# Four of eight output tiles stay in PSUM from one feed-forward round to the next

## The chip, the cores and the metric

One core of a Trainium2 chip runs the whole kernel. The metric is device time in microseconds (us). Five engines take part: TensorE (PE in the profile: matmuls; PEld is its weight load), VectorE (DVE), ScalarE (ACT), GpSimd (POOL) and SyncE (SP), which issues the loads of weights. Each has its own queue of instructions and runs it in order; they wait for each other by semaphores. Matmuls write to PSUM, which has eight banks of 512 float32 values per partition; `k.bank[0]` to `k.bank[7]` here.

## What is computed

Two blocks of a transformer on 512 tokens of width 1024, in float32: an "even" and an "odd" mixer, then a chain with four feed-forward stages and two mixers between them. Only the feed-forward stages (`ffn00`, `ffn01`, `ffn10`, `ffn11`) are touched:

```python
def swiglu(x, w_in, w_out):                       # w_in 1024 x 5632, w_out 2816 x 1024
    gate, up = jnp.split(x @ w_in, 2, axis=-1)
    return (jax.nn.silu(gate) * up) @ w_out
...
h = layer_norm(DN_ALPHA * h + 0.5 * swiglu(h, ffn_w_in[i, 0], ffn_w_out[i, 0]), ln_g[i, 0], ln_b[i, 0])
```

## The kernel before

**Precision.** Every float32 operand is held as a high part and the rest (`w_hi`, `w_lo`, `h_hi`, `h_lo`, ...), and each product is three matmuls (lines 368 to 370, or 448 to 450 for the output): high by high, high by rest, rest by high. ScalarE makes the high part by a copy, VectorE the rest by a subtraction of the high part from the value.

**Rounds.** A feed-forward stage goes over its 2816 hidden features in 11 rounds of 256 (`ROUNDS`). Round r has three pieces of weights: "a" and "b" (each 128 gate and 128 up columns of `w_in`) and "o" (256 rows of `w_out`). TensorE's order is a(r), b(r), and then the output of the round before, o(r-1). From round 2 (`SEVEN`) on, each of a and b is done by seven products of half-sized blocks instead of eight (`PRODUCTS`, `tensor_seven`): products x = 0 to 6, each of 12 matmuls of 256 columns, into banks 0 to 3. The weights that such a product takes come in three units: A22, A1 (blocks A11 and A12), and S, four sums of blocks. GpSimd makes the sums in four instructions (`gpsimd_sums`, lines 1076, 1078, 1079 and 1081, in this order), ScalarE their high part (line 1106), VectorE the rest in two halves (`vector_unit_s`, line 1130), and the second half raises `w_s`. GpSimd starts on the next piece's sums when the `w_s` of the piece before is raised and its weights have landed. `vector_unit_a22` is line 1123, `vector_unit_a1` line 1140.

**Between the products** VectorE adds partial results: `vector_mid` (lines 1150, 1153, and 1156 with 1157), `vector_c11` (1163), `vector_c12` (1169) and `vector_products` (1177, and 1182 twice). TensorE's product 4 waits for line 1150 (`f_u`), product 5 for line 1153 (`f_e`), product 6 for lines 1156 and 1157 (`f_g`). Line 1049 is the rest of one of four sums of the activations, made once a stage (`vector_t_rest`).

**The output.** `tensor_out` makes o(r) as eight tiles j of 128 tokens by 512 columns (`OUTS`), in banks 4 to 7: tile j in bank 4 + j % 4. A tile is six matmuls of 512 columns, three for each half of the hidden features. It first does the first half for tiles 0 to 3, then the second half tile by tile, and tiles 4 to 7 entirely, each after the tile before it in its bank has been taken out. VectorE takes each tile out and adds it onto `acc` (`vector_out`, line 544; line 542 in the round that also multiplies by ALPHA). The last two rounds of a stage (9 and 10) are made by `tensor_exit` on top of tiles copied back into PSUM. Neither it nor round 8's eight takes change.

**The order of VectorE's queue** is written out by hand in `vector_ffn` and `vector_seventh`. The places where tiles 4 to 7 are taken out are these:

```python
    vector_t_rest(k, stage, "T1")                       # vector_ffn, before round 2
    vector_outs_ffn(k, stage, 0, range(4, 8))
    vector_seventh(k, stage)                            # begins with vector_unit_a22, vector_mid, ...
...
    vector_unit_a22(k, n)                               # vector_seventh, before round 3
    vector_outs_ffn(k, stage, r - 1, range(4, 8))
    vector_unit_s(k, n, 0)
```

Of the kernel before, what the change touches and what calls it, by code (L numbers as in the profile page):

```python
# [24 lines left out]
ROUNDS = DFF // 256  # L25
# [93 lines left out]
PIECES = _pieces()  # L119
AT = {p: n for n, p in enumerate(PIECES)}  # L120
# [49 lines left out]
def seeded(n, j=0):  # L170


    stage, what, i = PIECES[n]
    if stage[:3] == "ffn":
        return what == "o" and i >= ROUNDS - 2
    last = i >= NH - 2 if stage == "gla" else i == NH - 1
    return stage in SEEDED and what in ("out", "oa", "ob") and last and j in SEEDED[stage]


def gated(n):  # L180
# [259 lines left out]
def out_part(k, n, j, c, first, last, hi, lo):  # L440
    return out_tile(k, n, j, c, k.bank[4 + j % 4][:], first, last, hi, lo)


def out_tile(k, n, j, c, o, first, last, hi, lo):
    t, half = OUTS[j]
    onto = seeded(n, j)
    x, w = slice(t * P, (t + 1) * P), slice(c * D + half * T, c * D + (half + 1) * T)
    k.nc.tensor.matmul(o, hi[:, c, x], k.hi(n)[:, w], start=first and not onto, stop=False, skip_group_check=onto)  # L448
    k.nc.tensor.matmul(o, lo[:, c, x], k.hi(n)[:, w], start=False, stop=False, skip_group_check=onto)  # L449
    return k.nc.tensor.matmul(o, hi[:, c, x], k.lo(n)[:, w], start=False, stop=last, skip_group_check=onto)  # L450


def tensor_out(k, n, ready, free, order=(0, 1), hi=None, lo=None):


    pe = k.nc.tensor
    hi, lo = (k.oh_hi, k.oh_lo) if hi is None else (hi, lo)
    pe.wait_ge(*k.at("w_lo", n))
    pe.wait_ge(*k.at(*ready[0]))
    for j in range(4):  # L460
        pe.wait_ge(*k.at(*free[j]))
        out_part(k, n, j, order[0], True, False, hi, lo)
    pe.wait_ge(*k.at(*ready[1]))
    for j in range(8):
        if j >= 4:
            pe.wait_ge(*k.at("acc", (n, j - 4)))
            out_part(k, n, j, order[0], True, False, hi, lo)
        ins = out_part(k, n, j, order[1], False, True, hi, lo)
        ins.then_inc(*(k.up("out", (n, j)) if j < 7 else k.up("used", n)))


def tensor_exit(k, B, n, ready, free, turn, free_turn, order=(0, 1), x=None, n0=None, ready0=(), x0=None):
# [56 lines left out]


def out_done(n, j):
    return ("out", (n, j)) if j < 7 else ("used", n)


def vector_out(k, n, j, alpha=False, bank=None):


    t, half = OUTS[j]
    dst, b = k.acc[:, t, half * T:(half + 1) * T], k.bank[4 + j % 4 if bank is None else bank][:]
    k.nc.vector.wait_ge(*k.at(*out_done(n, j)))  # L540
    if alpha:
        ins = k.nc.vector.scalar_tensor_tensor(dst, dst, ALPHA, b, MULT, ADD)
    else:
        ins = k.nc.vector.scalar_tensor_tensor(dst, b, 1.0, dst, MULT, ADD)  # L544
    ins.then_inc(*k.up("acc", (n, j)))
# [573 lines left out]
def vector_unit_a22(k, n):  # L1119
    ve = k.nc.vector  # L1120
    ve.wait_ge(*k.at("u_hi", (n, "A22")))
    hi, lo = (wide_view(x) for x in w_blocks(k, n, "A22", 1))
    ve.tensor_tensor(lo, raw_block(k, n, 1, 1), hi.bitcast(F32), SUB)
# [11 lines left out]
def vector_unit_a1(k, n):  # L1135

    ve = k.nc.vector
    ve.wait_ge(*k.at("u_hi", (n, "A1")))
    hi, lo = (wide_view(x) for x in w_blocks(k, n, "A1", 2))
    ve.tensor_tensor(lo, a1_raw(k, n), hi.bitcast(F32), SUB).then_inc(*k.up("w_lo", n))  # L1140
# [19 lines left out]
def vector_c11(k, stage, r, s):  # L1160
    ve, key, p1 = k.nc.vector, (stage, r, s), k.f_h[:, s, HALF[0]]
    ve.wait_ge(*k.at("f_p", key + (4,)))
    ve.tensor_tensor(p1, p1, k.bank[1][:, 0:256], ADD).then_inc(*k.up("f_c11", key))  # L1163
# [139 lines left out]
def vector_seventh(k, stage):  # L1303


    r = SEVEN
    n, n_o = AT[stage, "b", r], AT[stage, "o", r - 1]
    vector_unit_a22(k, n)
    vector_mid(k, stage, r, 0, 0)
    vector_mid(k, stage, r, 0, 1)  # L1310
    vector_unit_a1(k, n)
    vector_mid(k, stage, r, 0, 2)
    vector_c11(k, stage, r, 0)
    vector_unit_s(k, n, 0)
    vector_unit_s(k, n, 1)
    vector_c12(k, stage, r, 0)
    vector_piece_half(k, n_o, 0)
    vector_products(k, stage, r, 0)
    k.nc.vector.wait_ge(*k.at("f_h", (stage, r, 0)))
    vector_mid(k, stage, r, 1, 0)  # L1320
    vector_hidden_split(k, stage, r, 0)
    vector_mid(k, stage, r, 1, 1)
    vector_piece_half(k, n_o, 1)
    vector_mid(k, stage, r, 1, 2)
    n = AT[stage, "a", r + 1]
    vector_unit_a22(k, n)
    vector_c11(k, stage, r, 1)
    vector_c12(k, stage, r, 1)
    vector_products(k, stage, r, 1)
    vector_unit_s(k, n, 0)  # L1330
    vector_unit_s(k, n, 1)
    vector_hidden_split(k, stage, r, 1)
    vector_outs_ffn(k, stage, r - 1, range(2))
    vector_unit_a1(k, n)
    vector_outs_ffn(k, stage, r - 1, range(2, 4))
    n = AT[stage, "b", r + 1]
    vector_unit_a22(k, n)
    vector_outs_ffn(k, stage, r - 1, range(4, 8))
    vector_unit_s(k, n, 0)
    vector_unit_s(k, n, 1)  # L1340


def vector_ffn(k, stage):
    ve, B = k.nc.vector, FFN_NEXT[stage]
    vector_piece(k, AT[stage, "a", 1])
    ve.wait_ge(*k.at("h_lo", (stage, 1, 3)))
    vector_t_sum(k, stage, "T1")
    ve.wait_ge(*k.at("t_sum", (stage, "T1")))
    vector_t_sum(k, stage, "T2")
    vector_t_rest(k, stage, "T2")  # L1350
    vector_hidden(k, stage, 0, 0)
    vector_piece(k, AT[stage, "b", 1])
    vector_hidden_split(k, stage, 0, 0)
    ve.wait_ge(*k.at("t_lo", (stage, "T2")))
    vector_t_sum(k, stage, "T4")
    vector_t_rest(k, stage, "T4")
    vector_hidden(k, stage, 0, 1)
    vector_hidden_split(k, stage, 0, 1)
    vector_piece(k, AT[stage, "o", 0])
    ve.wait_ge(*k.at("t_lo", (stage, "T4")))  # L1360
    vector_t_sum(k, stage, "T3")
    vector_t_rest(k, stage, "T3")
    vector_hidden(k, stage, 1, 0)
    n = AT[stage, "a", SEVEN]
    vector_unit_a22(k, n)
    vector_hidden_split(k, stage, 1, 0)
    vector_hidden(k, stage, 1, 1)
    vector_outs_ffn(k, stage, 0, range(2))
    vector_unit_s(k, n, 0)
    vector_outs_ffn(k, stage, 0, range(2, 3))  # L1370
    vector_hidden_split(k, stage, 1, 1)
    vector_outs_ffn(k, stage, 0, range(3, 4))
    vector_unit_s(k, n, 1)
    vector_unit_a1(k, n)
    vector_t_rest(k, stage, "T1")
    vector_outs_ffn(k, stage, 0, range(4, 8))
    vector_seventh(k, stage)
    for r in range(SEVEN + 1, ROUNDS):
        last = r == ROUNDS - 1
        vector_mid(k, stage, r, 0, 0)  # L1380
        vector_piece(k, AT[stage, "o", r - 1])
        vector_mid(k, stage, r, 0, 1)
        vector_mid(k, stage, r, 0, 2)
        vector_unit_a1(k, AT[stage, "b", r])
        vector_c11(k, stage, r, 0)
        vector_c12(k, stage, r, 0)
        vector_products(k, stage, r, 0)
        vector_hidden_split(k, stage, r, 0)
        n = None if last else AT[stage, "a", r + 1]
        if not last:  # L1390
            vector_unit_a22(k, n)
        vector_mid(k, stage, r, 1, 0)
        vector_mid(k, stage, r, 1, 1)
        if last:
            vector_piece(k, AT[stage, "o", r])
        else:
            vector_unit_s(k, n, 0)
        vector_mid(k, stage, r, 1, 2)
        if not last:
            vector_unit_s(k, n, 1)  # L1400
        vector_c11(k, stage, r, 1)
        vector_c12(k, stage, r, 1)
        vector_products(k, stage, r, 1)
        vector_hidden_split(k, stage, r, 1)
        if not last:
            vector_outs_ffn(k, stage, r - 1, range(2))
            vector_unit_a1(k, n)
            vector_outs_ffn(k, stage, r - 1, range(2, 4))
            n = AT[stage, "b", r + 1]
            vector_unit_a22(k, n)  # L1410
            vector_unit_s(k, n, 0)
            vector_outs_ffn(k, stage, r - 1, range(4, 6))
            vector_unit_s(k, n, 1)
            vector_outs_ffn(k, stage, r - 1, range(6, 8))
        elif B != "end":
            vector_piece(k, HEAD[B][0])
            vector_piece(k, HEAD[B][1])
    vector_exit(k, B, AT[stage, "o", ROUNDS - 1])


def vector_outs_ffn(k, stage, r, outs):
    for j in outs:
        vector_out(k, AT[stage, "o", r], j, r == 0)


def sync_final(k):
# [2511 lines left out]
```

## Time and profile before

| | |
|---|---|
| time, median of 3 runs (lowest, highest) | 2694.2 us (2692.37, 2696.44) |
| time of the profiled execution | 2693.18 us |
| its span, first to last instruction | 2691.6 us |
| mean granted clock of TensorE | 0.997 |
| busy: PE, PEld | 2646.5 us (98%), 2303.0 us (86%) |
| busy: VectorE, ScalarE, GpSimd | 1937.9 us (72%), 1123.7 us (42%), 577.0 us (21%) |
| takes of line 544 and line 542 | 374 and 48 |

Times of rows are us from the start of the span. A row of the timeline gives start, duration, engine and line, and what it writes and reads; a number in brackets is the idle time of the engine before it and what ended it. Of a feed-forward stage's three pieces, products run on lines 368 to 370 of PE and outputs on lines 448 to 450.

### The profile page before, as it was taken

To read this page: it belongs to the slowest core of one execution; us is meant where nothing else is said; L and a number is where in the kernel's file an instruction comes from. 1 tells how busy PE (TensorE), PEld (TensorE's weight loads), DVE (VectorE), ACT (ScalarE), POOL (GpSimd) and SP (SyncE) were. 2 spreads that over 40 slices of the span, in tenths; PEclk is the share of its full clock that TensorE was granted. 3 is DMA by queue.
4 is the path that set the end of the run, shared out by engine and by line. 5 is a ranking of instruction groups with operands and counts; after the bars stand their busy time and mean duration, and the time that the engine had idled before them with its cause. 6 is when DMAs were issued, how large, how long until landed. Compare 5 with 4: busy or idle time off the path is not lost.

```text
span 2691.6 us, 38695 instructions
## 1 busy us (share of the span) xinstructions
PE 2646.5 (98%) x15901; PEld 2303.0 (86%) x15901; DVE 1937.9 (72%) x2651; ACT 1123.7 (42%) x1624; POOL 577.0 (21%) x366
## 2 busy tenths in 40 slices
PE   9899999999999999999999999999999999999998
PEld 6787877678899997888999988999988888889997
DVE  7888634656888865448888778888655745788876
ACT  4444555543433445353434444434432332444343
POOL 2211000101444400001544214444000000044440
PEclk9999999999999999999999999999999999999999
DMA  9543222212333332222333323333323223233331
GB/s 303 157 150 107 63 63 63 79 52 78 122 94 106 99 110 66 92 63 73 116 97 121 108 72 121 95 107 98 110 83 110 78 72 110 78 108 97 94 110 63
DMA packets 297891, 268.34 MB, mean 100 GB/s; under 512 B 11047, under 2 KB 265265, under 8 KB 297586
## 3 DMA queue, kind: packets, MB, share of 16 engines
q1 hardware_dynamic: 294050, 256.99, 30.9%
q0 software_dynamic: 2368, 6.64, 0.7%
q8 instruction: 126, 2.06, 0.3%
q10 hardware_dynamic: 1296, 2.23, 0.3%
q14 instruction: 51, 0.42, 0.0%
HBM read 263.72 MB, written 2.10 MB: 99 GB/s over the span
## 4 chain that ended last, share of the span: by engine, by line
PE 81%; DVE 12%; ACT 3%; issue 3%; POOL 1%; DMA 0%; DVEq 0%; POOLq 0%; ACTq 0%
PE psum L368 14%; PE psum L370 14%; PE psum L369 14%; PE psum L448 7%; PE psum L449 7%; PE psum L450 7%; PE psum L424 2%; PE psum L425 2%; PE psum L426 2%; PE psum L3040 1%; DVE w_lo L353 1%; DVE w_lo L1130 1%; PE psum L3053 1%; PE psum L1621 1%; PE psum L2608 1%
## 5 line engine op out<-in xcount | busy, mean ns | idle before, releaser
L368 PE MATMUL psum<-h_hi,w_hi 128*128 128x256 f32 (+1 forms) x2224 | 720.0, 324 | 12.8 <-DVE consts L1153 4.2
L370 PE MATMUL psum<-h_hi,w_lo 128*128 128x256 f32 (+1 forms) x2224 | 701.8, 316 | 0.0
L369 PE MATMUL psum<-h_lo,w_hi 128*128 128x256 f32 (+1 forms) x2224 | 701.4, 315 | 0.0
L368 PEld LDWEIGHTS psum<-h_hi,w_hi 128*128 128x128 f32 x2224 | 425.5, 191 | 47.7 <-issue 9.7
L369 PEld LDWEIGHTS psum<-h_lo,w_hi 128*128 128x128 f32 x2224 | 425.5, 191 | 28.4 <-issue 4.8
L370 PEld LDWEIGHTS psum<-h_hi,w_lo 128*128 128x128 f32 x2224 | 425.1, 191 | 27.0
L1076 POOL TENSOR_TENSOR val<-w_raw 128x512 f32<-128x512 f32 x72 | 100.4, 1395 | 963.5 <-DMA w_raw<-in_ffn_w_in 567.9
L353 DVE TENSOR_TENSOR w_lo<-w_raw,w_hi 128x2048 fp32r<-128x2048 f32 x98 | 223.1, 2287 | 83.4 <-ACT w_hi L348 77.3
L544 DVE SCALAR_TENSOR_TENSOR acc<-psum,acc 128x512 f32<-128x512 f32 x374 | 242.2, 679 | 36.0 <-PE psum L450 35.4
L368 PE MATMUL psum<-t_hiffn,w_hi 128*128 128x256 f32 x864 | 244.9, 283 | 0.4
L369 PE MATMUL psum<-t_loffn,w_hi 128*128 128x256 f32 x864 | 244.5, 283 | 0.0
L370 PE MATMUL psum<-t_hiffn,w_lo 128*128 128x256 f32 x864 | 244.5, 283 | 0.0
L348 ACT ACTIVATE w_hi<-w_raw 128x2048 fp32r<-128x2048 f32 x102 | 193.3, 1910 | 65.9 <-PE psum L450 57.2
L1200 ACT ACTIVATE consts<-consts 128x256 f32<-128x256 f32 x144 | 58.2, 418 | 294.6 <-DVE consts L1163 270.0
L1130 DVE TENSOR_TENSOR w_lo<-val,w_hi 128x1024 fp32r<-128x1024 f32 x144 | 174.1, 1216 | 9.4 <-ACT w_hi L1106 8.5
L368 PEld LDWEIGHTS psum<-t_hiffn,w_hi 128*128 128x128 f32 x864 | 165.8, 192 | 1.3 <-DVE f_cffn L1157 1.3
L369 PEld LDWEIGHTS psum<-t_loffn,w_hi 128*128 128x128 f32 x864 | 165.9, 192 | 0.0
L370 PEld LDWEIGHTS psum<-t_hiffn,w_lo 128*128 128x128 f32 x864 | 165.9, 192 | 0.0
L1079 POOL TENSOR_TENSOR val<-w_raw 128x512 f32<-128x512 f32 x72 | 161.4, 2241 | 0.0
L1106 ACT ACTIVATE w_hi<-val 128x2048 fp32r<-128x2048 f32 x72 | 138.0, 1916 | 38.0 <-POOL val L1081 31.2
L348 ACT ACTIVATE w_hiffn<-w_raw 128x2048 fp32r<-128x2048 f32 x40 | 76.5, 1913 | 128.3 <-PE psum L450 128.3
L448 PE MATMUL psum<-w_hiffn,f_oh_hiffn 128*128 128x512 f32 x320 | 125.6, 393 | 0.0
(460 smaller groups left out, 5603.0 us busy)
## 6 DMA issues: line engine op xcount, KB each, us to landing
w_raw<-in_ffn_w_in SPq DMA_DIRECT2D x176, 512.0 KB, 5.0
w_raw<-in_ffn_w_out SPq DMA_DIRECT2D x88, 512.0 KB, 6.2
w_raw<-in_ret_w_in SPq DMA_DIRECT2D x48, 512.0 KB, 4.6
ada_raw<-in_ada_w SPq DMA_DIRECT2D x32, 512.0 KB, 4.4
w_raw<-in_odd_w_in SPq DMA_DIRECT2D x32, 512.0 KB, 4.8
w_raw<-in_even_w_in SPq DMA_DIRECT2D x24, 512.0 KB, 6.1
w_raw<-in_gla_w_in SPq DMA_DIRECT2D x24, 512.0 KB, 4.8
ada_first<-in_ada_w SPq DMA_DIRECT2D x32, 256.0 KB, 6.2
```

Of the source, the lines that this page charges most:

```text
L348: k.nc.scalar.activation(k.hi(n), k.w_raw[:, buffer(n), :], ACT.Copy).then_inc(*k.up("w_hi", n))
L353: k.nc.vector.tensor_tensor(k.lo(n), k.w_raw[:, buffer(n), :], k.hi(n).bitcast(F32), SUB).then_inc(*k.up("w_lo", n))
L368: k.nc.tensor.matmul(out, ws, xs, start=first, stop=False)
L369: k.nc.tensor.matmul(out, ws, xl, start=False, stop=False)
L370: return k.nc.tensor.matmul(out, wl, xs, start=False, stop=last)
L448: k.nc.tensor.matmul(o, hi[:, c, x], k.hi(n)[:, w], start=first and not onto, stop=False, skip_group_check=onto)
L449: k.nc.tensor.matmul(o, lo[:, c, x], k.hi(n)[:, w], start=False, stop=False, skip_group_check=onto)
L450: return k.nc.tensor.matmul(o, hi[:, c, x], k.lo(n)[:, w], start=False, stop=last, skip_group_check=onto)
L544: ins = k.nc.vector.scalar_tensor_tensor(dst, b, 1.0, dst, MULT, ADD)
L1079: po.tensor_tensor(sum_block(k, "S3"), a11, a21, ADD).then_inc(*k.pool.up())
L1106: sc.activation(w_blocks(k, n, "S", 4)[0], k.sums, ACT.Copy).then_inc(*k.up("u_hi", (n, "S")))
L1130: ins = ve.tensor_tensor(lo, k.sums[:, x], hi.bitcast(F32), SUB)
```

## The change

Tiles of o(0) to o(7) are no longer all taken out. Each of these rounds leaves the last four tiles that it made in banks 4 to 7. The next round makes the same four tiles first and adds onto what lies there, so tiles alternate: round 0 goes 0 to 7 and keeps 4 to 7; round 1 goes 4 to 7, then 0 to 3, and keeps 0 to 3; and so on. VectorE takes out the first four of a round, in the same places of its queue as before, and four takes a round fall away for eight rounds. Round 8 begins with the four that were kept and has all eight taken out. TensorE's waits for the take of a kept tile fall away too. No matmul is added or removed.

```diff
--- before.py
+++ after.py
@@ -177,6 +177,23 @@
     return stage in SEEDED and what in ("out", "oa", "ob") and last and j in SEEDED[stage]
 
 
+def kept(r):
+
+    return r < ROUNDS - 3
+
+
+def out_order(n):
+
+    stage, what, r = PIECES[n]
+    return (4, 5, 6, 7, 0, 1, 2, 3) if stage[:3] == "ffn" and what == "o" and r < ROUNDS - 2 and r % 2 else tuple(range(8))
+
+
+def onto_kept(n, j):
+
+    stage, what, r = PIECES[n]
+    return stage[:3] == "ffn" and what == "o" and 0 < r < ROUNDS - 2 and kept(r - 1) and j in out_order(n)[:4]
+
+
 def gated(n):
     return PIECES[n][0] in ("even", "odd") and PIECES[n][1] == "out"
 
@@ -443,7 +460,7 @@
 
 def out_tile(k, n, j, c, o, first, last, hi, lo):
     t, half = OUTS[j]
-    onto = seeded(n, j)
+    onto = seeded(n, j) or onto_kept(n, j)
     x, w = slice(t * P, (t + 1) * P), slice(c * D + half * T, c * D + (half + 1) * T)
     k.nc.tensor.matmul(o, hi[:, c, x], k.hi(n)[:, w], start=first and not onto, stop=False, skip_group_check=onto)
     k.nc.tensor.matmul(o, lo[:, c, x], k.hi(n)[:, w], start=False, stop=False, skip_group_check=onto)
@@ -457,16 +474,18 @@
     hi, lo = (k.oh_hi, k.oh_lo) if hi is None else (hi, lo)
     pe.wait_ge(*k.at("w_lo", n))
     pe.wait_ge(*k.at(*ready[0]))
-    for j in range(4):
-        pe.wait_ge(*k.at(*free[j]))
+    tiles = out_order(n)
+    for j in tiles[:4]:
+        if not onto_kept(n, j):
+            pe.wait_ge(*k.at(*free[j % 4]))
         out_part(k, n, j, order[0], True, False, hi, lo)
     pe.wait_ge(*k.at(*ready[1]))
-    for j in range(8):
-        if j >= 4:
-            pe.wait_ge(*k.at("acc", (n, j - 4)))
+    for j in tiles:
+        if j not in tiles[:4]:
+            pe.wait_ge(*k.at("acc", (n, j ^ 4)))
             out_part(k, n, j, order[0], True, False, hi, lo)
         ins = out_part(k, n, j, order[1], False, True, hi, lo)
-        ins.then_inc(*(k.up("out", (n, j)) if j < 7 else k.up("used", n)))
+        ins.then_inc(*k.up(*out_done(n, j)))
 
 
 def tensor_exit(k, B, n, ready, free, turn, free_turn, order=(0, 1), x=None, n0=None, ready0=(), x0=None):
@@ -529,7 +548,7 @@
 
 
 def out_done(n, j):
-    return ("out", (n, j)) if j < 7 else ("used", n)
+    return ("out", (n, j)) if j != out_order(n)[-1] else ("used", n)
 
 
 def vector_out(k, n, j, alpha=False, bank=None):
@@ -1335,7 +1354,6 @@
     vector_outs_ffn(k, stage, r - 1, range(2, 4))
     n = AT[stage, "b", r + 1]
     vector_unit_a22(k, n)
-    vector_outs_ffn(k, stage, r - 1, range(4, 8))
     vector_unit_s(k, n, 0)
     vector_unit_s(k, n, 1)
 
@@ -1373,7 +1391,6 @@
     vector_unit_s(k, n, 1)
     vector_unit_a1(k, n)
     vector_t_rest(k, stage, "T1")
-    vector_outs_ffn(k, stage, 0, range(4, 8))
     vector_seventh(k, stage)
     for r in range(SEVEN + 1, ROUNDS):
         last = r == ROUNDS - 1
@@ -1409,9 +1426,11 @@
             n = AT[stage, "b", r + 1]
             vector_unit_a22(k, n)
             vector_unit_s(k, n, 0)
-            vector_outs_ffn(k, stage, r - 1, range(4, 6))
+            if not kept(r - 1):
+                vector_outs_ffn(k, stage, r - 1, range(4, 6))
             vector_unit_s(k, n, 1)
-            vector_outs_ffn(k, stage, r - 1, range(6, 8))
+            if not kept(r - 1):
+                vector_outs_ffn(k, stage, r - 1, range(6, 8))
         elif B != "end":
             vector_piece(k, HEAD[B][0])
             vector_piece(k, HEAD[B][1])
@@ -1419,8 +1438,9 @@
 
 
 def vector_outs_ffn(k, stage, r, outs):
+    n = AT[stage, "o", r]
     for j in outs:
-        vector_out(k, AT[stage, "o", r], j, r == 0)
+        vector_out(k, n, out_order(n)[j], r < 2 and j < 4)
 
 
 def sync_final(k):
```

## Rows read from the trace of the kernel before

**Rows 1.** The page: busy time of TensorE, and the costliest group of takes.

```profile
PE 2646.5 (98%) x15901; PEld 2303.0 (86%) x15901; DVE 1937.9 (72%) x2651; ACT 1123.7 (42%) x1624; POOL 577.0 (21%) x366
...
L544 DVE SCALAR_TENSOR_TENSOR acc<-psum,acc 128x512 f32<-128x512 f32 x374 | 242.2, 679 | 36.0 <-PE psum L450 35.4
```

**Rows 2.** Windows of ffn01: products of rounds 2, 3 and 4; length, busy times, clock, DMA.

```profile
1275.21:1296.74 21.53, 20.87 (x169) 20.39 (x169) 20.80 (x28) 10.07 (x12) 13.52 (x10) 1.00 0.57 164
...
1307.65:1329.37 21.72, 20.66 (x170) 20.25 (x168) 17.62 (x24) 9.86 (x12) 9.74 (x7) 1.00 0.33 103
...
1340.28:1360.43 20.15, 20.15 (x170) 20.15 (x168) 15.28 (x24) 8.21 (x11) 9.93 (x6) 1.00 0.36 112
```

**Rows 3.** TensorE's waits over the whole run: total us, times, longest.

```profile
PE psum L368 <- DVE consts L1153: 4.2, 4, 1.1
...
PE psum L368 <- DVE f_cffn L1150: 2.3, 4, 0.7
```

**Rows 4.** Timeline of TensorE in ffn01, at three places of rounds 2 and 3.

```profile
1279.51 0.28 PE L370 MATMUL psum<-h_hi,w_lo 128*128 128x256 f32 x1
...
1291.85 0.39 PE L368 MATMUL psum<-h_hi,w_hi 128*128 128x256 f32 x1 [0.54 <-DVE f_cffn L1150]
...
1316.04 0.39 PE L368 MATMUL psum<-h_hi,w_hi 128*128 128x256 f32 x1 [1.04 <-DVE consts L1153]
```

**Rows 5.** Timeline of VectorE in ffn01, start of round 2.

```profile
1275.08 2.33 DVE L1049 TENSOR_TENSOR h_lo<-lng,h_hi 128x1024 fp32r<-128x1024 f32 x1
1277.33 2.47 DVE L542 SCALAR_TENSOR_TENSOR acc<-acc,psum 128x512 f32<-128x512 f32 x4
1279.72 0.68 DVE L1123 TENSOR_TENSOR w_lo<-w_raw,w_hi 128x512 fp32r<-128x512 f32 x1
1280.32 0.41 DVE L1150 TENSOR_TENSOR f_cffn<-consts,psum 128x256 f32<-128x256 f32 x1
1280.83 0.42 DVE L1153 TENSOR_TENSOR consts<-f_cffn,psum 128x256 f32<-128x256 f32 x1
1281.17 1.47 DVE L1140 TENSOR_TENSOR w_lo<-w_raw,w_hi 128x1024 fp32r<-128x1024 f32 x1
...
1283.56 2.35 DVE L1130 TENSOR_TENSOR w_lo<-val,w_hi 128x1024 fp32r<-128x1024 f32 x2
```

**Rows 6.** Timeline of GpSimd in the same stretch.

```profile
1274.16 2.16 POOL L1076 TENSOR_TENSOR val<-w_raw 128x512 f32<-128x512 f32 x1 [24.10 <-DVE w_lo L1130]
1276.40 2.17 POOL L1078 TENSOR_TENSOR val<-val,w_raw 128x512 f32<-128x512 f32 x1
1278.53 1.31 POOL L1079 TENSOR_TENSOR val<-w_raw 128x512 f32<-128x512 f32 x1
1279.92 1.64 POOL L1081 TENSOR_TENSOR val<-val,w_raw 128x512 f32<-128x512 f32 x1
```

**Rows 7.** Timeline of ScalarE in the same stretch.

```profile
1281.59 1.92 ACT L1106 ACTIVATE w_hi<-val 128x2048 fp32r<-128x2048 f32 x1 [0.34 <-POOL val L1081]
```

**Rows 8.** Timeline of VectorE in ffn01, later in round 2.

```profile
1291.38 0.42 DVE L1150 TENSOR_TENSOR f_cffn<-consts,psum 128x256 f32<-128x256 f32 x1
```

**Rows 9.** Timeline of VectorE in ffn01, from o(1) into round 3.

```profile
1305.08 2.10 DVE L544 SCALAR_TENSOR_TENSOR acc<-psum,acc 128x512 f32<-128x512 f32 x3
1307.85 0.69 DVE L544 SCALAR_TENSOR_TENSOR acc<-psum,acc 128x512 f32<-128x512 f32 x1 [0.67 <-PE psum L450]
1309.68 2.36 DVE L1130 TENSOR_TENSOR w_lo<-val,w_hi 128x1024 fp32r<-128x1024 f32 x2 [1.14 <-ACT w_hi L1106]
...
1312.29 3.36 DVE L353 TENSOR_TENSOR w_loffn<-w_raw,w_hiffn 128x2048 fp32r<-128x2048 f32 x1
```

**Rows 10.** Timeline of GpSimd in ffn01: the last sum for round 3.

```profile
1306.41 1.29 POOL L1081 TENSOR_TENSOR val<-val,w_raw 128x512 f32<-128x512 f32 x1
```

**Rows 11.** Timelines of VectorE and GpSimd in ffn01, into round 4.

```profile
1343.35 0.42 DVE L1150 TENSOR_TENSOR f_cffn<-consts,psum 128x256 f32<-128x256 f32 x1 [0.87 <-PE psum L370]
...
1341.65 1.32 POOL L1076 TENSOR_TENSOR val<-w_raw 128x512 f32<-128x512 f32 x1 [8.51 <-DMA w_raw<-in_ffn_w_in]
```

## Prediction

> **What bounds the kernel now.** I read the page first. TensorE's matmuls are busy for 98% of the span [rows 1], so the question is where TensorE stands still in the four feed-forward stages; only such time can be given back, since the change leaves every matmul in place. All matmuls of one size follow each other at one fixed spacing, so a stretch of TensorE with a known count of matmuls has a known length, and what is over it is a stall. I cut ffn01 into windows at the points where TensorE goes from lines 368-370 to 448-450 and back. The products of round 4 take 20.15 us, with TensorE busy all the time; the timeline of the later rounds looks the same. Round 2 takes 21.53 us and round 3 21.72 us for the same products [rows 2]. So a stage loses 1.38 us in round 2 and 1.57 us in round 3, 2.95 us, some 12 us in four stages. The waits of TensorE confirm who is late: lines 1150 and 1153 of VectorE, four times each, once a stage [rows 3]. In the timeline the first is product 4 of b in round 2, which waits for line 1150, the second product 5 of a in round 3, which waits for line 1153 [rows 4].
>
> **What is removed, and what it is worth by itself.** Eight rounds of four takes in four stages are 128 takes at 0.679 us [rows 1], 87 us of VectorE's time. In rounds 4 to 10 TensorE doesn't wait, so nothing comes of it there. The takes matter only in so far as they make VectorE late for the two stalls. Both have four of them somewhat ahead in VectorE's queue.
>
> **Round 3 first.** VectorE's last take ends at 1307.85 + 0.69 = 1308.54. Then it stands still for 1.14 us until ScalarE has made the high part of S, and starts on S at 1309.68 [rows 9]. ScalarE had waited for GpSimd's last sum, which runs from 1306.41 to 1307.70 in 1.29 us, under takes [rows 10]; its other durations in this stage are 1.31 us at the least and 2.17 us at the most [rows 6]. So takes don't slow GpSimd, and without them S would start at 1309.68 all the same. The next piece, line 353, is held to 3.36 us and is what makes line 1153 late [rows 9, 4]; it comes behind S and doesn't move. Removing the four takes here is worth 0: what hides them is the wait for GpSimd's sums.
>
> **Round 2.** Here four takes at 1277.33 to 1279.80 stand between line 1049 and line 1123 [rows 5]. They are covered in the same way: S starts at 1283.56 [rows 5], 0.05 us after ScalarE's line 1106 has ended at 1281.59 + 1.92 = 1283.51, which began 0.03 us after GpSimd's last sum ended at 1279.92 + 1.64 = 1281.56 [rows 6, 7]. So also here the earlier VectorE gains nothing past S. The sums themselves, however, can get later.
>
> Look at how the two engines run against each other. GpSimd's 1076 takes 2.16 us, 1078 2.17, 1079 1.31 and 1081 1.64 [rows 6]. 1079 is the one that runs wholly beside takes. 1078 was issued at 1276.40 while VectorE's line 1049 was running until 1275.08 + 2.33 = 1277.41, and ended 1.16 us after that. Line 1049 in turn was issued while GpSimd's 1076 ran until 1276.32, and ended 1.09 us after that, though the same shape on line 1130 takes 2.35 / 2 [rows 5]. So the two do not share: a subtraction of VectorE that reads two operands from SBUF and a sum of GpSimd run one after the other, and they take turns, where both stand ready. A take, which reads one operand from PSUM, doesn't count, and nor do lines 1150 and 1153.
>
> The Trainium skill says it so ("SBUF — State Buffer", "Who interferes with whom"): VectorE and GpSimd share a port pair under an exclusive lock for the whole instruction, and a VectorE instruction with two SBUF inputs contends with a GpSimd instruction that reads SBUF, one with at most one SBUF input doesn't. The trace agrees with it: 1.31 us beside takes, 2.17 us beside line 1049. This rule speaks against the change: the takes are a stretch in which GpSimd has the port for itself. The same page ("A bandwidth-pool intuition that's wrong") gives some 115 ns from the end of the one to the start of the other, for a DMA issue held by a copy; with three handovers more on GpSimd's way (below) that would be an estimate of 0.35 us a stage, and the sum 1.4 us higher.
>
> Now without the takes, step by step for ffn01:
> - line 1123 is issued at 1277.33, just as GpSimd's 1078 has got its turn, which it holds until 1276.40 + 2.17 = 1278.57. An instruction that was held ends its own length less 0.13 us after the other (1.22 against 1.09 for line 1049), so 1123 ends at 1278.57 + 0.68 - 0.13 = 1279.12.
> - 1079 is issued at 1278.53 as before, is now held by 1123, and ends 1.16 us after it, at 1280.28. Before: 1279.84.
> - line 1150 runs from 1279.04. Line 1153 needs product 2, whose last matmul starts at 1279.51 and lasts 0.28 us [rows 4]. So it starts at some 1279.83, and line 1140 is issued 0.34 us later, at 1280.17. 1081 can't be issued before 1280.36 (1079's end and the 0.08 us seen between them now). So 1140 is next in turn and ends 1.09 us after 1079, at 1281.37.
> - 1081 ends 1.16 us after that, at 1282.53, in place of 1281.56: 0.97 us later.
> - ScalarE's 1106 follows 0.03 us later, and S 0.05 us after it: 1284.53 in place of 1283.56.
>
> Behind S in VectorE's queue stand line 1169, half of line 360, 1177, 1182 twice and line 1150 at 1291.38 [rows 8], which TensorE has waited for since product 3 of b was issued; GpSimd's next sums are started by the end of S, so they move with it and meet the same instructions. None of these waits for TensorE, and nothing between gives the time back. So line 1150 and TensorE's restart at 1291.85 [rows 4] move by 0.97 us, and all that follows in the stage moves with TensorE. Three other stages have the same order and the same durations. **Sum:** 4 x 0.97 = +3.9 us.
>
> **The other parts of the change.** Accumulating in place of overwriting: the second half of each tile accumulates today at the same spacing, so 0. The other order of tiles: the same 48 matmuls, the first four of a round still taken in the same places, so 0. The waits dropped for kept tiles: these takes ended at 1308.54, 20 us before the next output at 1329.37, so 0 (its cover is a whole round). From round 4 on S ends some 1.2 us earlier, which raises `w_s` earlier; but GpSimd's first sum waits for its weights to land (1341.65, after 8.51 us), and line 1150 waits for TensorE (1343.35) [rows 11]. So these meet as before: 0. Below nothing I see no cost here, unless the load lands earlier than I read it, which is a rival below.
>
> **Against the measured time.** The profiled execution took 2693.18 us with a span of 2691.6 us, 1.6 us around it; it is 1.0 us below the median of 2694.2 us. I add the sum to the median: **2698.1 us**. A difference under 0.2% (5.4 us) is about what a measurement of this kernel can't tell from no change, and the forecast lies within it.
>
> **Rivals.**
> - *The turn falls the other way* (0.22). Line 1140 is issued only 0.19 us ahead of 1081. If it comes later, 1081 goes first and ends 1.25 us after its issue at 1280.36, at 1281.61 in place of 1281.56. Then nothing moves: 2694.2 us, within 1. For it speaks how small the margin is, against it that all of it hangs on TensorE's regular spacing.
> - *The stalls go* (0.12), the case on the other side. If what holds S back is VectorE's lateness and not the sums, then VectorE comes to both places 2.4 us earlier (four takes of 2.47 us), more than either stall. All of it: -4 x 2.95 = -11.8 us, 2682.4 us (0.04). Only round 3's: -4 x 1.57 = -6.3 us, 2687.9 us (0.05); less than that, 2691 us (0.03). It decides from where the sums end more than 1 us ahead of VectorE's arrival at S. Against it stand the 0.03 and 0.05 us of rows 5 to 7 and the 1.14 us of idle time in rows 9.
> - *A new collision in rounds 4 to 10* (0.08). If the weights land early enough that GpSimd starts 1.2 us sooner, its sums meet line 353 in another phase, and a whole sum of 1.3 us can come ahead of it. In rows 11 GpSimd is let go by the load, so it is unlikely. The price lies between 0 and the 1.31 us of a sum; TensorE has some slack in these rounds, so I take 0.5 us, in six rounds of four stages +12 us: 2706 us. It decides from line 1153 being later than product 4 of a takes.
> - *The forecast* (0.58): 2695.5 to 2700.5 us, the handovers' price being the unknown.
>
> **How the numbers follow.** The range reaches from the half-way gains to the forecast's upper end with some of the costly case: 2689 to 2702 us. Faster by over 0.2%: the first two parts of the second rival, 0.09. Slower by over 0.2%: the third rival and the upper edge of the forecast, 0.08 + 0.08 = 0.16. Within: 0.75.
>
> **What the profile after would show.** If right: 246 takes of line 544 in place of 374 (and 48 of line 542, as now, since round 1's first four are scaled in place of round 0's last); line 1079 of round 2 at some 1.75 us in place of 1.31, and 1081 at 2.2 in place of 1.64; S of round 2 a microsecond later against TensorE's start of the round; products of round 2 at 22.5 us, of round 3 at 21.7, of round 4 at 20.15. It is wrong if round 3's products fall to 20.2 us, or if round 2's stay at 21.5 us.

## The result and the profile after

The changed kernel takes 2698.49 us (median of 20 runs, 2694.35 to 2701.92) against 2694.38 us for the kernel before (20 runs, 2691.77 to 2697.28). The ratio is 1.0016, with a 95% interval of 1.0009 to 1.0023: slower by 4.1 us, forecast +3.9.

The page of the changed kernel: its VectorE line, and the group of takes.

```profile
PE 2651.5 (98%) x15901; PEld 2306.7 (85%) x15901; DVE 1867.4 (69%) x2523; ACT 1122.5 (42%) x1624; POOL 581.1 (22%) x366
...
L563 DVE SCALAR_TENSOR_TENSOR acc<-psum,acc 128x512 f32<-128x512 f32 x246 | 160.1, 680 | 32.8 <-PE psum L467 32.7
```

VectorE is busy for 70.5 us less than in [rows 1], with 128 instructions fewer, and TensorE makes the same 15901 matmuls. (The 128 takes lasted 87 us, but the rows of neighbouring takes overlap a little, and VectorE's other instructions last 6.3 us longer in all: one that is held by another engine counts as busy.) The kernel is slower all the same. Windows of the same three stretches of ffn01 say where; columns as in [rows 2].

```profile
1279.33:1301.84 22.51, 21.13 (x170) 20.48 (x169) 19.43 (x24) 9.85 (x12) 14.47 (x10) 1.00 0.53 159
1312.75:1334.20 21.45, 20.40 (x169) 20.20 (x168) 16.56 (x23) 9.74 (x12) 9.65 (x7) 1.00 0.33 105
1345.14:1365.29 20.15, 20.15 (x169) 20.15 (x168) 13.34 (x22) 8.18 (x11) 9.92 (x6) 1.00 0.37 115
```

Round 2 has grown from 21.53 to 22.51 us, round 4 is 20.15 us as it was. Cut in the same way, round 2 takes 22.50, 22.51, 22.50 and 22.49 us in the four stages, 3.7 us more in all than the 21.66, 21.53, 21.57 and 21.55 us before. Round 3 gives 0.3 us back in one stage. TensorE's waits over the whole run:

```profile
PE psum L385 <- DVE f_cffn L1169: 5.0, 4, 1.3
PE psum L385 <- DVE consts L1172: 4.2, 4, 1.0
```

Lines 1169 and 1172 are lines 1150 and 1153 of before. The wait for the first has gone from 2.3 to 5.0 us in total, that for the second has stayed at 4.2 us [rows 3]. The rows of waits show less than the windows do (2.7 against 3.7 us), since a part of each stall counts as busy: for the same matmuls of round 2 the busy time has gone from 20.87 to 21.13 us. The windows are what I go by. The profiled execution of the changed kernel took 2701.88 us, 8.7 us more than that of before, and only 3.4 us of this lie in rounds 2 and 3. Another 3.3 us lie ahead of the first instruction that differs (its round 2 of ffn00 begins at 689.20 us, before at 685.94 us), and 1.9 us between round 3 of ffn10 and round 2 of ffn11, where TensorE's granted clock fell to 1.2 GHz for some 3 us in this execution (the last section shows it). A single pair of spans would have told more than twice the truth; medians and stretches of fixed work agree.

**How the microsecond is lost.** VectorE in ffn01, start of round 2, after:

```profile
1279.19 2.34 DVE L1068 TENSOR_TENSOR h_lo<-lng,h_hi 128x1024 fp32r<-128x1024 f32 x1
1281.45 1.78 DVE L1142 TENSOR_TENSOR w_lo<-w_raw,w_hi 128x512 fp32r<-128x512 f32 x1
1283.16 0.41 DVE L1169 TENSOR_TENSOR f_cffn<-consts,psum 128x256 f32<-128x256 f32 x1
1283.95 0.42 DVE L1172 TENSOR_TENSOR consts<-f_cffn,psum 128x256 f32<-128x256 f32 x1 [0.39 <-PE psum L387]
1284.29 1.22 DVE L1159 TENSOR_TENSOR w_lo<-w_raw,w_hi 128x1024 fp32r<-128x1024 f32 x1
...
1286.83 0.42 DVE L1182 TENSOR_TENSOR consts<-consts,psum 128x256 f32<-128x256 f32 x1 [0.67 <-PE psum L387]
1288.64 2.36 DVE L1149 TENSOR_TENSOR w_lo<-val,w_hi 128x1024 fp32r<-128x1024 f32 x2 [1.39 <-ACT w_hi L1125]
...
1296.46 0.42 DVE L1169 TENSOR_TENSOR f_cffn<-consts,psum 128x256 f32<-128x256 f32 x1
```

GpSimd and ScalarE beside it, and TensorE at product 4 of b:

```profile
1280.52 2.16 POOL L1097 TENSOR_TENSOR val<-val,w_raw 128x512 f32<-128x512 f32 x1
1282.65 1.77 POOL L1098 TENSOR_TENSOR val<-w_raw 128x512 f32<-128x512 f32 x1
1284.50 2.17 POOL L1100 TENSOR_TENSOR val<-val,w_raw 128x512 f32<-128x512 f32 x1
```

```profile
1286.70 1.91 ACT L1125 ACTIVATE w_hi<-val 128x2048 fp32r<-128x2048 f32 x1 [1.33 <-POOL val L1100]
```

```profile
1296.93 0.39 PE L385 MATMUL psum<-h_hi,w_hi 128*128 128x256 f32 x1 [1.24 <-DVE f_cffn L1169]
```

Line 1142 (1123 before) has the same work as in [rows 5] and lasts 1.78 us in place of 0.68, because it stands behind sum 1097. The third sum lasts 1.77 us in place of 1.31, behind line 1142, and the fourth 2.17 us in place of 1.64, behind line 1159. VectorE, which was busy almost without a gap up to S before, now stands still for 0.39, for 0.67 and, ahead of S, for 1.39 us, and S is still later. The removed work was replaced by waiting, and the waiting is longer.

### The profile page after: what moved, and what is told of

Same layout as the page of the kernel before. It is cut to its first block, busy times and chain, and to the rows that moved or that the text cites. A ratio compares the mean times of both kernels' runs of the same rounds, so it can differ in the third digit from the quotient of the medians.

```text
span 2700.3 us, 38567 instructions
## 1 busy us (share of the span) xinstructions
PE 2651.5 (98%) x15901; PEld 2306.7 (85%) x15901; DVE 1867.4 (69%) x2523; ACT 1122.5 (42%) x1624; POOL 581.1 (22%) x366
## 4 chain that ended last, share of the span: by engine, by line
PE 79%; DVE 12%; ACT 4%; issue 3%; POOL 2%; DMA 0%; DVEq 0%; SPq 0%; POOLq 0%; ACTq 0%
PE psum L385 13%; PE psum L387 13%; PE psum L386 13%; PE psum L465 7%; PE psum L466 7%; PE psum L467 7%; PE psum L443 2%; PE psum L441 2%; PE psum L442 2%; DVE w_lo L370 1%; PE psum L3060 1%; DVE w_lo L1149 1%; PE psum L3073 1%; PE psum L1641 1%; PE psum L2628 1%
## 5 line engine op out<-in xcount | busy, mean ns | idle before, releaser
L563 DVE SCALAR_TENSOR_TENSOR acc<-psum,acc 128x512 f32<-128x512 f32 x246 | 160.1, 680 | 32.8 <-PE psum L467 32.7
```

## Experiments

Two theories of the loss. **A**, that of the prediction: in round 2 GpSimd's sums lose turns to VectorE's subtractions, since the four takes beside which they ran undisturbed are gone. **B**: every kept round costs TensorE a little, by accumulating onto a bank or by the other order of tiles; 4.1 us over 32 kept rounds is 0.13 us each, too little to be told from a few products. They differ in where the loss sits and in whether it can be undone with all kept tiles in place.

**Only round 0 keeps tiles** (`e1`). In every later round all eight tiles are taken out as before, though the odd rounds stay in the other order of tiles:

```diff
 def kept(r):
-    return r < ROUNDS - 3
+    return r == 0
...
 def evacuated(n):
-    return [("acc", (n, 4 + j)) for j in range(4)]
+    return [("acc", (n, out_order(n)[4 + j])) for j in range(4)]
...
     vector_unit_a22(k, n)                               # vector_seventh, before round 3
+    vector_outs_ffn(k, stage, r - 1, range(4, 8))
     vector_unit_s(k, n, 0)
```

> Only round 0 of each stage keeps its last four tiles; round 1 makes them first and then all eight are taken out, and the later rounds are as before. Theory A (the sums of round 2 lose their turns at the port once the four takes of round 0 are gone): all of the loss is here, +3.9 us against before, products of round 2 at 22.5 us in place of 21.5. Theory B (each kept round costs something on TensorE, by accumulating or by its other order): one of eight kept rounds, +0.5 us, round 2 at 21.5 us.

Measured: 2698.71 us against 2694.91, ratio 1.0013 (1.0005 to 1.0022). Its round 2 in ffn01:

```profile
1277.02:1299.54 22.52, 21.13 (x169) 20.46 (x169) 19.44 (x24) 9.86 (x12) 14.50 (x10) 1.00 0.54 158
```

16 of the 128 removed takes bring the whole loss, as theory A has it.

**All rounds but round 0 keep tiles** (`e2`), with the changed `evacuated` too:

```diff
 def kept(r):
-    return r < ROUNDS - 3
+    return 0 < r < ROUNDS - 3
...
     vector_t_rest(k, stage, "T1")                       # vector_ffn, before round 2
+    vector_outs_ffn(k, stage, 0, range(4, 8))
     vector_seventh(k, stage)
...
-        vector_out(k, n, out_order(n)[j], r < 2 and j < 4)
+        vector_out(k, n, out_order(n)[j], r == 0)
```

> Rounds 1 to 7 keep four tiles, round 0 doesn't: its last four takes are back ahead of round 2. Theory A: no change against before, within 1 us, products of round 2 at 21.5 us and of round 3 at 21.4 to 21.7 us, though 112 of the 128 takes are gone. Theory B: seven of eight kept rounds, +3.6 us.

Measured: 2694.62 us against 2694.91, ratio 1.0000 (0.9991 to 1.0008). Windows of its rounds 2 and 3 in ffn01:

```profile
1274.36:1295.92 21.56, 20.88 (x169) 20.39 (x169) 20.82 (x28) 10.07 (x12) 13.53 (x10) 1.00 0.55 164
1306.83:1328.54 21.71, 20.66 (x169) 20.25 (x168) 16.93 (x23) 9.86 (x12) 9.73 (x7) 1.00 0.33 104
```

Removing the other 112 takes is worth nothing that could be measured, and accumulating onto a kept bank in seven rounds costs nothing either: every output of 48 matmuls takes 10.91 us, as before. Theory B, which asked for 3.6 us, falls. Round 3's own stall is there (21.71 us), though the four takes just ahead of its S are gone: their cover was GpSimd, as [rows 9, 10] said.

**The turns given back, with every tile kept** (`e3`). One line moves in `vector_seventh`:

```diff
-    vector_unit_a22(k, n)
     vector_mid(k, stage, r, 0, 0)
+    vector_unit_a22(k, n)
     vector_mid(k, stage, r, 0, 1)
```

> The changed kernel with one line moved: in round 2 VectorE adds the first partial result (vector_mid 0) ahead of the rest of A22, and no longer behind it. The partial result is ready only when TensorE has done product 1, so the rest of A22 is issued some 0.2 us after GpSimd's third sum and not 1.2 us ahead of it. Theory A: the third sum falls back from 1.77 to 1.3 us, the fourth ends a microsecond earlier, round 2's products return to 21.5 us, and the time to that of before, within 1 us (-4 us against the changed kernel). Theory B: the time stays at +4 us.

Measured: 2694.14 us against 2694.91, ratio 0.9999 (0.9990 to 1.0008). VectorE and GpSimd in its ffn01:

```profile
1276.27 0.42 DVE L1169 TENSOR_TENSOR f_cffn<-consts,psum 128x256 f32<-128x256 f32 x1 [0.99 <-PE psum L387]
1276.60 1.67 DVE L1142 TENSOR_TENSOR w_lo<-w_raw,w_hi 128x512 fp32r<-128x512 f32 x1
```

```profile
1276.40 1.32 POOL L1098 TENSOR_TENSOR val<-w_raw 128x512 f32<-128x512 f32 x1
1277.80 1.64 POOL L1100 TENSOR_TENSOR val<-val,w_raw 128x512 f32<-128x512 f32 x1
```

```profile
1273.08:1294.64 21.56, 20.90 (x170) 20.42 (x169) 19.93 (x24) 10.08 (x12) 13.52 (x10) 1.00 0.56 165
```

VectorE makes the same instructions as in the changed kernel, but line 1142 is now issued 0.20 us after the third sum and not 1.2 us ahead of it. The sums last 1.32 and 1.64 us, as in [rows 6], and round 2 is back at 21.56 us. The order of two instructions carries the whole loss.

**What the idle time can be used for** (`e4`). TensorE waits for what stands in VectorE's queue behind S, and the changed kernel has a hole ahead of S. Half of the subtraction for the output weights fits in:

```diff
     vector_c11(k, stage, r, 0)
+    vector_piece_half(k, n_o, 0)
     vector_unit_s(k, n, 0)
     vector_unit_s(k, n, 1)
     vector_c12(k, stage, r, 0)
-    vector_piece_half(k, n_o, 0)
```

> The changed kernel, with the first half of the rest of the output weights (vector_piece_half 0) moved ahead of S in round 2, into the 2 us in which VectorE now stands still for the sums. Theory A with the chain behind S as what TensorE waits for: S is no later, line 1150 (1169 in the changed kernel) comes some 2.2 us earlier, product 4 of b no longer waits, products of round 2 fall from 22.5 to 20.2 to 20.5 us, and the time to some 2689.5 us, 5 us under before. If VectorE's place behind S isn't what holds TensorE, nothing moves and it stays at +4 us.

Measured: 2691.40 us against 2694.91, ratio 0.9988 (0.9979 to 0.9996), and round 2 at 21.08 us in ffn01. The sign is right, but round 2 was expected at 20.2 to 20.5 us, so some 0.6 to 0.9 us a stage are missing. TensorE in ffn01 at product 6 of b, and what it waited for:

```profile
1293.11 0.28 PE L387 MATMUL psum<-h_hi,w_lo 128*128 128x256 f32 x1
1293.69 0.39 PE L385 MATMUL psum<-t_hiffn,w_hi 128*128 128x256 f32 x1 [0.30 <-DVE f_cffn L1176]
```

```profile
1290.65 0.41 DVE L1172 TENSOR_TENSOR consts<-f_cffn,psum 128x256 f32<-128x256 f32 x1
1290.98 1.99 DVE L377 TENSOR_TENSOR w_loffn<-w_raw,w_hiffn 128x1024 fp32r<-128x1024 f32 x1
1292.90 0.41 DVE L1175 TENSOR_TENSOR f_cffn<-consts,psum 128x256 f32<-128x256 f32 x1
1293.23 0.41 DVE L1176 TENSOR_TENSOR f_cffn<-f_cffn,psum 128x256 f32<-128x256 f32 x1
```

The wait for line 1169 is gone, and the next one behind it shows: the second half (line 377) is held to 1.99 us by a sum and stands ahead of the partial result for product 6. I had followed the chain to product 4 and no further.

**Both halves moved** (`e6`): besides the edit above,

```diff
     vector_mid(k, stage, r, 1, 1)
-    vector_piece_half(k, n_o, 1)
     vector_mid(k, stage, r, 1, 2)
+    vector_piece_half(k, n_o, 1)
```

> The changed kernel with both halves of the rest of the output weights moved in round 2: the first ahead of S, the second behind vector_mid 2 of b. In the run before, with only the first moved, product 6 of b still lost some 0.5 us behind the second half and product 1 of b 0.2 us behind S. If that reading is right, round 2's products take 20.4 us (21.1 with the first half alone, 22.5 without), round 3's stay at 21.4 to 21.7, and the time is some 2690 us, 4.6 us under before. If product 6 waits for something else, 21.1 us stays.

Measured: 2690.44 us against 2695.39, ratio 0.9981 (0.9972 to 0.9990), round 2 at 20.53 us and round 3 at 21.71 us in ffn01, as expected to 0.1 us. What keeps round 2 some 0.4 us above 20.15 us was not followed up.

**Round 3 as well** (`e7`), in the loop of `vector_ffn`:

```diff
         vector_mid(k, stage, r, 0, 0)
-        vector_piece(k, AT[stage, "o", r - 1])
+        n_o, third = AT[stage, "o", r - 1], r == SEVEN + 1
+        if not third:
+            vector_piece(k, n_o)
         vector_mid(k, stage, r, 0, 1)
+        if third:
+            vector_piece_half(k, n_o, 0)
         vector_mid(k, stage, r, 0, 2)
...
         vector_mid(k, stage, r, 1, 0)
+        if third:
+            vector_piece_half(k, n_o, 1)
         vector_mid(k, stage, r, 1, 1)
```

> As the kernel with both halves moved, and in round 3 too line 353 (370) is cut into halves: the first behind vector_mid 1 of a, the second behind vector_mid 0 of b. What made TensorE wait in round 3 was this one long instruction, held by GpSimd's first sum, ahead of the partial result for product 5. Round 3's products fall from 21.4 to 21.7 us to 20.2 to 20.6, round 2's stay at 20.4, and the time is some 2685.5 us, 9 us under before. If VectorE has too much to do in round 3 for another order to help, the wait comes back at a later product and 21.4 us or more stays.

**And the same moves in the kernel before** (`e8`), with all its takes:

> The kernel before (all 128 takes in place) with the same moves in rounds 2 and 3. It says what the kept tiles are worth once VectorE's order is right. If the takes are covered in round 3 and cost at most a little ahead of S in round 2, where the half piece now comes on top of them, round 2's products take 20.6 to 21.0 us and round 3's 20.2 to 20.6, the time is some 2686.5 to 2687.5 us, and the kept tiles are worth 1 to 2 us. If VectorE's load is what counts, round 2 stays above 21.4 us and the gap to the run above is over 4 us.

Measured: `e7` 2686.66 us, ratio 0.9968 (0.9959 to 0.9977); `e8` 2687.22 us, ratio 0.9974 (0.9966 to 0.9983); both against 2695.39 us. Windows of rounds 2 and 3 in ffn01, first `e7`, then `e8`:

```profile
1274.23:1294.73 20.50, 20.45 (x169) 20.28 (x169) 18.45 (x24) 9.88 (x12) 13.99 (x10) 1.00 0.52 160
1305.64:1325.79 20.15, 20.15 (x169) 20.15 (x168) 16.43 (x24) 9.64 (x12) 8.02 (x6) 1.00 0.36 113
```

```profile
1271.96:1292.63 20.67, 20.47 (x169) 20.30 (x169) 19.80 (x28) 10.00 (x12) 13.01 (x10) 1.00 0.59 158
1303.54:1323.69 20.15, 20.15 (x169) 20.15 (x168) 17.12 (x25) 9.62 (x12) 8.03 (x6) 1.00 0.37 114
```

The products of round 3 have lost their stall in both, so VectorE had time enough there for what they wait for; it did it in the wrong order. The windows of the products don't show that a part of the stall has moved behind them. The outputs after round 3, o(2), take longer; here they are before and in `e7`:

```profile
1329.37:1340.28 10.91, 10.91 (x51) 9.02 (x49) 9.98 (x14) 3.91 (x4) 3.69 (x3) 1.00 0.30 84
1325.79:1337.24 11.45, 11.22 (x51) 8.94 (x49) 10.52 (x12) 3.95 (x5) 4.49 (x4) 1.00 0.26 69
```

The two instructions that finish the hidden features (line 1182 before, 1201 in `e7`) now meet GpSimd's sums in another phase and last longer, and a take that TensorE waits for comes later. The first row is of before, the others are of `e7`:

```profile
1330.03 1.96 DVE L1182 SCALAR_TENSOR_TENSOR consts<-consts,f_cffn 128x256 f32<-128x256 f32 x2
...
1326.45 2.84 DVE L1201 SCALAR_TENSOR_TENSOR consts<-consts,f_cffn 128x256 f32<-128x256 f32 x2
1326.25 1.29 POOL L1097 TENSOR_TENSOR val<-val,w_raw 128x512 f32<-128x512 f32 x1
1331.65 0.50 PE L465 MATMUL psum<-w_hiffn,oh_hi 128*128 128x512 f32 x1 [0.23 <-DVE acc L563]
```

It is so in all four stages of both kernels (11.42 to 11.45 us). In `e7` the products of rounds 2 and 3 give back 10.2 us over the four stages, and these outputs take 2.1 us of it again, which leaves 8.2 us. The times say 8.7 us for `e7` and 8.2 us for `e8`. Between the two kernels lie 0.17 us in round 2 of this stage, some 0.7 us over four, which the intervals of their times don't tell apart; 1 to 2 us had been expected. That is about what the kept tiles are worth once the order is right.

## Why the prediction was right, step by step

- **What TensorE can give back.** Windows of equal work showed 2.95 us of stalls in two rounds of a stage, some 12 us in all [rows 2]. `e7` got 1.03 us of round 2 and 1.57 us of round 3 back in ffn01, and its products from round 3 on take 20.15 to 20.21 us, though 0.54 us came back as a stall in the outputs behind round 3. These 12 us were no part of the sum, only of the second rival.
- **The takes are covered in round 3.** Shown by `e2`, where round 3 took 21.71 us without them.
- **The takes are covered in round 2, and what they cover gets later.** The walk through ffn01 can be laid over the trace. From TensorE's first matmul of round 2 (1275.21 before, 1279.33 after), forecast and measured: line 1123 or 1142 ends at 3.91 and 3.90 us; the third sum ends at 5.07 and 5.09; line 1140 or 1159 is issued at 4.96 and 4.96; the fourth sum ends at 7.32 and 7.34; S starts at 9.32 and 9.31; TensorE restarts at 17.61 and 17.60. So the price of a handover, taken from one pair of rows before, carried over.
- **The Trainium skill's rule** ("SBUF — State Buffer", "Who interferes with whom") is what the runs show: where a VectorE subtraction with two SBUF inputs and a GpSimd sum meet, the second does its work after the first (1.78 us for line 1142 in place of 0.68), while a sum beside takes is not slowed (1.29 to 1.31 us in [rows 6, 10]). The estimate by its figure of 115 ns would have given 5.3 us; the measured loss of 4.1 us (the ratio's interval is 2.4 to 6.2 us) doesn't exclude it, but the places above fit the rows' handovers to 0.02 us.
- **The turn that could have fallen the other way.** Line 1159 was issued 0.21 us ahead of the fourth sum, forecast 0.19, in ffn01, and round 2 came out at the longer length in all four stages.
- **Accumulating, tile order, dropped waits, rounds 4 to 10:** all costed at 0, and none shows a cost: `e2` is at the time of before within 0.1%, and all products from round 4 on take 20.15 to 20.21 us. The collision that was a rival there didn't come: GpSimd's first sum still waited for its weights.
- **What was off:** 4 x 0.97 = 3.9 us was taken for four stages with the same durations. Round 2's own windows give 0.84, 0.98, 0.93 and 0.94 us, 3.7 us. In ffn00 before, S had started 8.45 us after TensorE's first matmul and not 8.35, and not because of the sums: ScalarE's high part was done 0.13 us ahead of it, and S stood right behind line 1163, so VectorE itself was late there and there was less to lose. With round 3's 0.3 us taken off, the windows give 3.4 us and the medians 4.1; the interval holds both, and the forecast's 3.9 us lies between them by chance. The first rival's 1.25 us for a sum that isn't held stands in no row either; the shortest is 1.29 us, and nothing hangs on the difference.
- **What the time alone doesn't show.** The stated range, 2689 to 2702 us, also holds the time of no change, and the 0.2% that the prediction took for the limit of what can be told apart was too wide: with 20 runs of each kernel 4.1 us stood clear of 0. What bears the mechanism out is the walk above and `e1` to `e3`.

## What to carry to other kernels

An instruction off the critical path may be keeping another one away from a shared resource. Before work is taken out of a queue, read what runs beside it on the other engines, and who moves into its place. Where an engine is in the way, ask first which instructions stand ahead of the awaited one, and whether they need to: here reordering a few instructions in two rounds of a stage took 8.2 us off the kernel before, while removing 128 instructions cost 4.1 us in the old order and gained nothing that could be measured in the new one. And look behind the stretch that was cured: a part of the stall can reappear there.

## What the runs showed of the hardware

- When VectorE and GpSimd stand ready within 0.01 us of each other, either can win. In round 3 of ffn01, before, GpSimd's third sum ran ahead of line 1140:

```profile
1316.75 1.30 POOL L1079 TENSOR_TENSOR val<-w_raw 128x512 f32<-128x512 f32 x1
...
1316.76 2.38 DVE L1140 TENSOR_TENSOR w_lo<-w_raw,w_hi 128x1024 fp32r<-128x1024 f32 x1
```

In the changed kernel it is the other way round:

```profile
1321.87 1.22 DVE L1159 TENSOR_TENSOR w_lo<-w_raw,w_hi 128x1024 fp32r<-128x1024 f32 x1
```

```profile
1321.86 2.39 POOL L1098 TENSOR_TENSOR val<-w_raw 128x512 f32<-128x512 f32 x1
```

It goes with round 3 taking 21.45 in place of 21.72 us, and not in this stage alone. The seven kernels that leave round 3's order as it was have 28 such rounds between them: the 8 in which VectorE's subtraction isn't held (1.22 us) take 21.43 to 21.46 us, the 20 in which it is (2.38 to 2.40 us) take 21.71 to 21.74. That the one makes the other was not tested by a change.
- TensorE's granted clock can fall in one execution and not in another at the same place of the work. Between ffn10 and ffn11 in the changed kernel, over the stretch in which TensorE stood still twice, for 1.19 and 1.54 us, the mean clock is 0.94, and in the 3.0 us behind the second pause, from 2312.97 to 2316.00, it is 0.50, the lower level of 1.2 GHz:

```profile
2300.00:2330.00 30.00, 27.27 (x130) 22.80 (x129) 21.45 (x32) 14.75 (x28) 1.09 (x2) 0.94 0.37 105
```

  The kernel before had 1.00 over the same stretch of its work, with pauses of 1.19 and 1.54 us too. With the first 690 us, which differ by up to 4.6 us from one profiled execution to the next (round 2 of ffn00 begins between 684.59 and 689.20 us in the nine profiles), this would be enough for the spread of 5.5 us between the runs of the kernel before; that it is its cause is not shown.
